# GpSimd sums for the last product of two memory layers, and new orders in the memory and last layers of a transformer kernel

## What is computed

```python
def memory_cross_attention(h, mem, wq, wkv, wo):
    q = (h @ wq).reshape(b, s, MEM_HEADS, MEM_HEAD_DIM)          # 4 heads of 256
    kv = (mem @ wkv).reshape(b, m, 2, MEM_HEADS, MEM_HEAD_DIM)
    k, v = kv[:, :, 0], kv[:, :, 1]
    sc = jnp.einsum('bqhd,bkhd->bhqk', q, k).astype(jnp.float32) * (MEM_HEAD_DIM ** -0.5)
    p = jax.nn.softmax(sc, axis=-1).astype(v.dtype)
    o = jnp.einsum('bhqk,bkhd->bqhd', p, v).reshape(b, s, D_MODEL)
    return o @ wo
...
for l in range(DEPTH):
    mix = hybrid_mixer(h, w_in[l], ...)
    h = layer_norm(ALPHA * h + mix, ln_g[l, 0], ln_b[l, 0])
    xa = memory_cross_attention(h, mem, mem_wq[l], mem_wkv[l], mem_wo[l])
    h = layer_norm(ALPHA * h + xa, ln_g[l, 1], ln_b[l, 1])
    f = swiglu(...) if l % 2 == 0 else moe_swiglu(...)
    h = layer_norm(ALPHA * h + f, ln_g[l, 2], ln_b[l, 2])
...
for layer in range(DEPTH):
    y = even_mixer(rmsnorm(x, pre_norm[layer]), ...) if layer % 2 == 0 else odd_mixer(...)
    x = x + rmsnorm(y, post_norm[layer])
```

## Time and profile before

| what | value |
|---|---|
| median of 3 runs (2184.64 to 2188.2) | 2184.92 us |
| the profiled execution | 2184.75 us, its span 2183.0 us |
| PE busy | 2119.3 us, 97% of the span, 13136 records (two for each matmul) |
| DVE, ACT, POOL busy | 677.9, 296.4, 64.9 us |
| granted clock of PE over the span | 0.993 |
| DMA | 485.52 MB, 222 GB/s on average |
| idle of PE in front of instructions | 14.5 us behind the norms of L1576, none other over 4.8 |

### The profile page before, as it was taken

How to read it: one execution, slowest core, us unless ns; L and a number is a source line. 1 busy time by engine, 2 the same in 40 slices (tenths; PEclk the granted TensorE clock), 3 DMA queues, 4 the chain that set the end, 5 groups by cost and what they waited for, 6 DMA issues and landing times.

```text
span 2183.0 us, 29181 instructions
## 1 busy us (share of the span) xinstructions
PE 2119.3 (97%) x13136; PEld 1240.2 (57%) x13136; DVE 677.9 (31%) x1278; ACT 296.4 (14%) x635; POOL 64.9 (3%) x70
## 2 busy tenths in 40 slices
PE   7999999999999999989999999999999899999997
PEld 3887675998458766743333334333333454755986
DVE  2413212455632241232101001111000389344445
ACT  1242001111103310010000000000000032330100
POOL 0000000000000000000000000000000025000000
PEclk9999999999999999989999999999999999999999
DMA  7523532544335244146999998799999832316340
GB/s 283 226 78 139 208 120 86 219 155 157 124 134 198 97 174 174 39 173 247 385 399 382 399 394 359 290 400 384 399 391 397 342 135 97 109 70 246 116 155 20
DMA packets 38000, 485.52 MB, mean 222 GB/s; under 512 B 4288, under 2 KB 4320, under 8 KB 6768
## 3 DMA queue, kind: packets, MB, share of 16 engines
q1 hardware_dynamic: 34544, 465.70, 53.5%
q0 software_dynamic: 3328, 17.90, 2.1%
HBM read 482.53 MB, written 1.05 MB: 222 GB/s over the span
## 4 chain that ended last, share of the span: by engine, by line
PE 95%; DVE 3%; DMA 1%; ACT 1%; issue 0%; DVEq 0%; SPq 0%
PE bank L362 51%; PE pair L362 44%; DMA weights<-in_w_in 0%; DVE att L1515 0%; DMA norm_par<-in_norms 0%; DVE hT L1515 0%; ACT hT L2545 0%; DVE att L2262 0%; ACT big L2529 0%; DVE stats L1567 0%; DVE h L1576 0%; DVE weights L2014 0%; DVE big L1515 0%; DVE h L1574 0%; DVE big L2244 0%
## 5 line engine op out<-in xcount | busy, mean ns | idle before, releaser
L362 PE MATMUL bank<-weights,att 128*32 128x512 f32 (+1 forms) x4228 | 459.6, 593 | 0.0
L362 PEld LDWEIGHTS bank<-weights,att 128*32 128x32 f32 (+1 forms) x4228 | 135.8, 110 | 307.4 <-issue 307.4
L362 PE MATMUL pair<-weights,big 128*32 128x512 f32 (+2 forms) x1654 | 249.1, 584 | 2.2 <-issue 2.2
L362 PE MATMUL bank<-hT,weights 128*128 128x256 f32 (+1 forms) x1168 | 239.1, 363 | 0.0
L362 PEld LDWEIGHTS bank<-hT,weights 128*128 128x128 f32 x1168 | 204.6, 190 | 31.4 <-issue 8.0
L362 PEld LDWEIGHTS pair<-weights,big 128*32 128x32 f32 (+1 forms) x1654 | 93.4, 122 | 146.1 <-issue 144.0
L362 PE MATMUL pair<-weights,hT 128*128 128x512 f32 (+2 forms) x400 | 167.5, 579 | 3.1 <-DMA weights<-in_w_in 1.6
L1910 DVE TENSOR_TENSOR big<-head_gain,bank 128x256 f32<-128x256 f32 x66 | 27.8, 421 | 423.9 <-ACT head_gain L2706 423.9
L362 PE MATMUL pair<-hT,weights 128*128 128x128 f32 (+1 forms) x976 | 154.6, 319 | 4.8 <-DVE hT L1515 3.9
L362 PEld LDWEIGHTS pair<-hT,weights 128*128 128x128 f32 x976 | 142.0, 194 | 16.6 <-DVE hT L1515 4.4
L362 PEld LDWEIGHTS pair<-weights,hT 128*128 128x128 f32 x400 | 76.5, 192 | 90.2 <-issue 86.2
(11 more groups left out here) (385 smaller groups left out, 1861.8 us busy)
## 6 DMA issues: line engine op xcount, KB each, us to landing
weights<-in_moe_up SPq DMA_DIRECT2D x88, 2048.0 KB, 10.6
weights<-in_moe_down SPq DMA_DIRECT2D x40, 2048.0 KB, 11.2
weights<-in_w_in SPq DMA_DIRECT2D x18, 2048.0 KB, 8.2
weights<-in_ffn_up SPq DMA_DIRECT2D x11, 2048.0 KB, 7.3
weights<-in_even_in SPq DMA_DIRECT2D x10, 2048.0 KB, 7.6
weights<-in_mem_wkv SPq DMA_DIRECT2D x8, 2048.0 KB, 7.3
weights<-in_odd_in SPq DMA_DIRECT2D x8, 2048.0 KB, 7.3
norm_par<-in_norms POOLq DMA_DIRECT2D x10, 1024.0 KB, 7.5
```

The lines of the kernel that those rows point to most:

```text
L362: ins = pe.matmul(o, lhsT, rhs, **flags)
```

## The change

1. In the memory layers kT1, v0, qT0 and qT1 are made by `seven_products`, with token sums in `prob` and `probT` and tile sums in the free part of `big`. hT is copied by ACT, not DVE. Scores wait for the half of qT that they need.
2. xo is made by `seven_rows`, whose seven sub-products have the rows as outputs; its token sums are made by DVE behind each head's value copy, and the sums over its two weight tiles by GpSimd (`xo_weight_sums`): eight subtractions of 128x1024, one after the other, from the end of qT1 on.
3. Its sums and norm are those of the dense layer's end, now a function (`rows_added`).
4. In the heads DVE's loop is written out, with the scaling of head 2 ahead of the value copy of head 0.
5. `few_sum` takes the last rows' statistics half by half.
6. Even layer: the turns and angles of step 0 come early, the scan's C is prepared in `prob` and `probT`, and two filler matmuls stand ahead of the wait for eu.
7. Odd layer: tile 14's sums are made once PE has finished the first half of c = 0, statistics and gain go by 256 columns, and for c = 1 the seventh sub-product has its own bank and is added ahead of the fourth.

```diff
...
+        xo_sums = [big_flat[:, 4096 + 2048 * i:6144 + 2048 * i].rearrange("p (r n) -> p r n", n=512) for i in range(3)]
+        xo_tokens = hT_flat.rearrange("p (i r t) -> p i r t", i=4, t=P)
...
-                for c in range(2):
-                    product_T(("kT", l, c), lambda kk: memT[:, kk, :], KD)
-                product(("v0", l), memT_at, KD, [512], KD)
+                product_T(("kT", l, 0), lambda kk: memT[:, kk, :], KD)
+
+                def memT_half(j, t):
+                    return lambda k: memT_at(KD // 2 * j + k, t)
+                seven_products(("kT", l, 1), memT_half, mem_sums, mem_tile_sums[1], first=True)
+                seven_products(("v0", l), memT_half, mem_sums, mem_tile_sums[0], by_token=True)
                 pe.wait_ge(*L.next("normed", 2))
-                transpose_rows(("hT", "mem", l), lambda t, kk: h[:, t, kk * P:(kk + 1) * P], KD)
-
-                pe.wait_ge(*emptied((("hT", "mem", l), KD - 2)))
-                for c in range(2):
-                    product_T(("qT", l, c), lambda kk: hT[:, kk, :], KD)
-                pe.wait_ge(*emptied(("qT", l, 1)))
+                transpose_rows(("hT", "mem", l), h_at, KD)
+                pe.wait_ge(*emptied((("hT", "mem", l), 2)))
+                seven_products(("qT", l, 0), hT_half, mem_sums, mem_tile_sums[1], first=True,
+                               second=lambda: pe.wait_ge(*emptied((("hT", "mem", l), KD - 2))))
+                seven_products(("qT", l, 1), hT_half, mem_sums, mem_tile_sums[0])
 
                 last_v = product_in_steps(("v", l), memT_at, KD, [512], 2)
 
                 def values(i):
                     def v(j):
+                        if (i, j) == (0, 0):
+                            pe.wait_ge(*emptied(("v0", l)))
                         if (i, j) == (MEM_HEADS // 2, 0):
                             pe.wait_ge(*emptied((("v", l), 0)))
                         return memory[:, j, i * MEM_HD:(i + 1) * MEM_HD]
                     return v
                 heads(("x", l), [([(hv[:, 2 * i + j, :], hv[:, 8 + 2 * i + j, :]) for j in range(2)],
-                                  values(i), MEM_HD, False) for i in range(MEM_HEADS)], last_v)
+                                  values(i), MEM_HD, False) for i in range(MEM_HEADS)], last_v,
+                      before=lambda i: pe.wait_ge(*emptied(("qT", l, i // 2))) if i in (0, 2) else None)
                 pe.wait_ge(*emptied((("x", l), "value", 3)))
-                product_rows(("xo", l), yT_at)
+                seven_rows(("xo", l), yT_at, xo_sums, xo_tokens, "xo_sums_ready")
...
+            def seven_rows(name, rows, sums, tokens_of, ready):
+
+                outs = rows_accumulators(name)
+                left, right = next_tile(), next_tile()
+                lt, rt = [weights[:, s, :].rearrange("p (r k n) -> p r k n", k=2, n=512) for s in (left, right)]
+                for i in (1, 2, 6, 5, 3, 7, 4):
+                    if i == 6:
+                        pe.wait_ge(*L.next(ready))
+                        pe.wait_ge(*L.next("xo_weights_ready"))
+                    for r in range(4):
+                        a11, a12, a21, a22 = [rows(2 * r + x, t) for t in range(NT) for x in range(2)]
+                        s1, s2, s3, s4 = [tokens_of[:, x, r, :] for x in range(4)]
+                        t1, t2, t4 = [t[:, r, :] for t in sums]
+                        tokens, block = {1: (a11, lt[:, r, 0, :]), 2: (a12, lt[:, r, 1, :]), 3: (s4, rt[:, r, 1, :]),
+                                         4: (a22, t4), 5: (s1, t1), 6: (s2, t2), 7: (s3, rt[:, r, 0, :])}[i]
+                        ins = mm(outs[i], tokens, block, start=(r == 0), stop=(r == 3))
+                    end_late(ins, (name, i))
+                    if i == 2:
+                        slot_owed[0] = f"slot{left}_used"
+                slot_owed[0] = f"slot{right}_used"
...
+                filling[0] = ("scan", 0)
+                fill(2)
...
-                    fill(4)
+                    fill(4 if b else 2)
...
+                    seventh = begin(banks, ("do", c, "seventh"), late=True)[:, 0:256] if c else last[:, 0:256]
...
+                                elif i == 4:
+                                    ins.then_inc(sems("do_half_done"), 1)
...
+                base = (first_ffn_tile + HID_CHUNKS + len(FEW_DOWN) if l else 0) + first_mem_tile
+
...
+                def summed(src):
+                    sums_of_tokens(src, mem_sums).then_inc(sems("token_sums_ready"), 1)
+                    L.passed("token_sums_ready")
+
+                def ahead(i):
+                    return lambda: sums_of_tile(tile(i), mem_tile_sums[i % 2])
+                memT = big_flat[:, 2048:4096].rearrange("p (k t) -> p k t", t=T)
+                ve.wait_ge(*emptied((("memT", l), KD - 2)))
+                ahead(1)()
+                summed(memT)
+                copy(("kT", l, 0), hv[:, 8:12, :].rearrange("p (a b) t -> p a (b t)", a=2))
+                crossed_tile(("kT", l, 1), mem_kept, lambda t, i: hv[:, 12 + 2 * i:14 + 2 * i, t * P:(t + 1) * P], ahead(2))
+                crossed_tile(("v0", l), mem_kept, lambda t, i: memory[:, t, 256 * i:256 * i + 256], ahead(3))
+                ve.wait_ge(*emptied((("hT", "mem", l), KD - 2)))
+                summed(hT)
+                crossed_tile(("qT", l, 0), mem_kept, lambda t, i: hv[:, 2 * i:2 * i + 2, t * P:(t + 1) * P], ahead(4))
+                crossed_tile(("qT", l, 1), mem_kept, lambda t, i: hv[:, 4 + 2 * i:6 + 2 * i, t * P:(t + 1) * P])
+                def token_sums_of(m):
+
+                    a11, a12, a21, a22 = [yT[:, 2 * m + x, t * P:(t + 1) * P] for t in range(NT) for x in range(2)]
+                    s1, s2, s3, s4 = [xo_tokens[:, i, m, :] for i in range(4)]
+                    link(ve.tensor_tensor(s1, a21, a22, ALU.add))
+                    link(ve.tensor_tensor(s2, s1, a11, ALU.subtract))
+                    ve.tensor_tensor(s3, a11, a21, ALU.subtract)
+                    return ve.tensor_tensor(s4, a12, s2, ALU.subtract)
 
                 def store(name, m):
                     copy(name, yT[:, 2 * m:2 * m + 2, :], lambda o: o[:, :].rearrange("p (k t) -> p k t", t=T))
-                heads(("x", l), MEM_HEADS, store, MEM_HD ** -0.5)
-                residual_norm(("xo", l))
+                    ve.wait_ge(*emptied(name))
+                    ins = token_sums_of(m)
+                    if m == MEM_HEADS - 1:
+                        ins.then_inc(sems("xo_sums_ready"), 1)
+                        L.passed("xo_sums_ready")
+                name = ("x", l)
+                heads_max(name, 0, MEM_HD ** -0.5)
+                heads_max(name, 1, MEM_HD ** -0.5)
+                heads_scaled(name, 0)
+                heads_max(name, 2, MEM_HD ** -0.5)
+                heads_scaled(name, 1)
+                heads_scaled(name, 2)
+                store((name, "value", 0), 0)
+                heads_max(name, 3, MEM_HD ** -0.5)
+                heads_scaled(name, 3)
+                for m in range(1, MEM_HEADS):
+                    store((name, "value", m), m)
+                rows_added(("xo", l), norm_slot(), ALPHA)
...
             def few_sum(g, row=None):
...
+                        if row is not None:
                             ve.wait_ge(*emptied(("few_sum", g, i, t)))
+                            ins = ve.bn_stats(stats[:, t, i, :], hc)
...
+            def rows_added(name, par, alpha=1.0):
 
...
-                def add(t, c, src, done=link):
-                    done(ve.tensor_tensor(part(t, c), part(t, c), src, ALU.add))
+                def add(t, c, src, done=link, scale=1.0):
+                    done(ve.scalar_tensor_tensor(part(t, c), part(t, c), scale, src, ALU.mult, ALU.add))
 
...
                 x, k1 = d_kept
...
-                row_norm(0, g, b)
-                add(1, 1, second[:, 0, :], freeing("B"))
-                ve.wait_ge(*filled((name, "down", 7)))
+                row_norm(0, *par)
+                add(1, 1, second[:, 0, :], freeing("B"), scale=alpha)
+                ve.wait_ge(*filled((name, 7)))
                 freeing(7)(ve.tensor_tensor(x, x, p7, ALU.add))
                 add(1, 1, x)
                 ve.bn_stats(stats[:, 1, 1, :], part(1, 1))
-                add(1, 0, x)
-                ve.wait_ge(*filled((name, "down", 4)))
+                add(1, 0, x, scale=alpha)
+                ve.wait_ge(*filled((name, 4)))
                 add(1, 0, p4, freeing(4))
                 link(ve.bn_stats(stats[:, 1, 0, :], part(1, 0)))
-                row_norm(1, g, b)
+                row_norm(1, *par)
...
+                ve.wait_ge(*L.next("do_half_done"))
+                sums_of_tile(odd_tile(14), do_tile_sums[0], "do_sums_ready")
...
+                    else:
+                        measured(0, c, 1)
...
+                        ve.wait_ge(*filled(("do", c, 7)))
+                        seventh, _ = bank(("do", c, "seventh"))
```

(39 more changed lines are left out.)

257 lines of the change are left out of this document (128 added, 129 removed).

## The result

The changed kernel takes 2162.03 us (median of 4 runs, 2160.9 to 2163.08) beside 2185.39 us for the kernel before (4 runs, 2184.64 to 2188.2): a ratio of 0.9891, 95% interval 0.9874 to 0.9908, so 23.4 us less. The forecast was 2156.2 with a range of 2150 to 2168. Direction and range held; 5.8 us of the expected gain are missing. (The profiled execution of the changed kernel, 2160.9 us, was its quickest; that is the other 1.1.)

What follows compares the result with a forecast made beforehand. TensorE (PE) was taken as the bound, 95% of the chain that ended last. Memory layers 25.4, less 4.0 for GpSimd's contention, plus 0.6, 2.1 and 4.4, made 28.5 us off 2184.75: 2156.2 us, range 2150 to 2168.

Steps and rivals of the forecast that it cites:

- Products and gaps ahead of the heads: Memory layers before the scores: seven products save 1.25 us each on kT1, qT0, qT1 and 1.65 on v0; gaps shrink too.
- The gap before qT: Memory layer, between v0 and qT: 1.8 us gained of the 1.96 us gap on VectorE.
- xo: Last product of each memory layer: 28 matmuls in place of 32, saving 3.45 us.
- The gaps in the heads: Memory layer, end of the heads: of gaps of 1.58 and 0.78 us, 1.3 gained.
- The sums by GpSimd: Memory layers: subtractions hidden from xo, but holding up VectorE in the heads 0 to 6 us a layer; 4.0 lost in all.
- three signs of being wrong: Memory layers: GpSimd's rows over 4.7 us, heads taking more than 34 us, or the clock falling inside the heads.
- first rival: Heads: every small VectorE instruction waits for a whole GpSimd one, 6 us a layer, clock falls too; 2168 us, chance 0.20.
- third rival: Whole kernel: no contention between GpSimd and VectorE, all gaps gone; 2150 us, chance 0.08.
- the second row's norm: After xo: norm takes about 5.8 us against 4.75, a gap of 2.7 before the second router transposes; 1.1 lost once.
- The expert layer's end: Last rows' statistics taken as each half is added: 0.6 us gained of PE's gap of 4.81.
- the even layer: Its start: the 2.31 us wait for eu goes, VectorE and GpSimd then bind the scan; 2.1 us gained (0.9 to 4.2).
- the last layer: The 2.68 us gap goes and the work behind the last matmul falls from 5.35 to 3.6 us; 4.4 gained.

Runs made afterwards that it cites:

- e10: The changed kernel with kT1, v0, qT0 and qT1 as before (eight products, hT copied by VectorE, scores waiting for all of qT): 2177.01 us.
- e1: The changed kernel with GpSimd's eight subtractions per memory layer left out, so some of xo's sub-products multiply other numbers: 2150.73 us.
- e6: The changed kernel with the scaling of the maximum made by ScalarE instead of VectorE, GpSimd's sums where they were: 2151.21 us.
- e9: The changed kernel with GpSimd's sums as four subtractions of 128x2048 per memory layer, rows doubled: 2163.65 us.
- e4: The changed kernel with GpSimd's eight subtractions of 128x1024 cut into sixteen of 128x512: 2153.01 us.
- e5: The changed kernel run again unchanged, as the base on another chip: 2161.48 us, a ratio of 0.9877 to the kernel before.
- e3: The changed kernel with xo's weight sums made by VectorE instead of GpSimd, five within qT1's time, three behind head 0's maximum: 2150.08 us.
- e12: e3 with six more matmuls of 128x512, results overwritten, ahead of xo in the first memory layer: 2157.82 us.
- e8: The changed kernel with three orders as before (last statistics of the experts, even layer's start, last layer): 2170.06 us.
- e2: The changed kernel with GpSimd's sums begun one tile earlier, five beside qT1 and three behind it: 2150.89 us.

## Why the prediction was right in its direction and 5.8 us short

**Products and gaps ahead of the heads: right.** 12.5 and 12.09 us per tile, forecast 12.51 and 12.09; 8.89 us a layer, forecast 8.52. The gap before qT went whole (1.96, taken as 1.8). e10 prices both layers' products alone.

**xo: right** in its size (3.43, forecast 3.45), and its sums were ready in time: GpSimd ended at 335.6, xo's third sub-product began at 357.6, 22 us later. The rows took 2.35 us, forecast 2.24, far from the 4.7 at which PE would have waited.

**The gaps in the heads: 1.3 forecast, 1.86 measured** (32.16 before, 30.30 in e1).

**The sums by GpSimd: the step that failed is the price of what they do to VectorE.** Two of the prediction's three signs of being wrong came: the heads took 35.03 us, over its 34, and in the second layer the clock fell inside them (below). That the time lies in the range does not make this step right. The working had all parts: two waits per head if the scaling of the maximum waits too, 1.5 us spare, 0 to 6 a layer. It then took 2, "nearer the lower end, as the row with two inputs is the only kind the trace shows waiting". Measured is 4.73 a layer in the first (30.30 in e1, 35.03 with the sums; the gaps are 4.29 of it, the rest is the overlap of matmuls lost at each stop). e6 shows that one term: without the small instruction nearly the whole loss goes, though prob still waits 2 us. The two waits add up, and a fixed amount of the sum is spare:

| head | wait of the small one | wait of prob | sum | PE's gap | spare |
|---|---|---|---|---|---|
| changed kernel, head 1 | 2.01 | 2.16 | 4.17 | 2.51 | 1.66 |
| changed kernel, head 2 | 1.28 | 2.16 | 3.44 | 1.78 | 1.66 |
| e9, head 1 | 1.48 | 4.31 | 5.79 | 4.13 | 1.66 |
| e10, head 1 | 0.43 | 2.17 | 2.60 | 0.94 | 1.66 |
| e4, head 1 | 0.37 | 1.08 | 1.45 | none | |
| e5, second layer, head 2 | 2.05 | 0 | 2.05 | 0.35 | 1.70 |
| changed kernel, second layer, head 2 | 0 | 1.96 | 1.96 | 0.31 | 1.65 |

A wait is the instruction's length less its length undisturbed, 0.17 or 0.69. The estimate of 1.5 spare was close, and one wait per head, as the forecast had it, costs 0.3 to 0.5 us; the second wait is what it left out. So the right reading was close to the first rival's condition (every small instruction waits for a whole GpSimd one; the tensor_scalar does, the reciprocal does not), at 4.7 a layer instead of its 6, and the measured 2162 lies in the span of that rival, 2160 to 2168, to which I gave 0.20, above the 2152 to 2160 of the forecast. The lack of a row for an instruction was taken as a reason for the low end, and it is none. The third rival, without contention, had 2150 us; the kernels in which VectorE waits for nothing take 2150.1 to 2150.9 (e1 to e3).

The rule of the Trainium skill that the prediction cited (SBUF — State Buffer, Who interferes with whom) names tensor_scalar among the instructions that can take the pair of ports shared with GpSimd, and tensor_reduce as one that never contends. The rows agree on both: 2.18 instead of 0.17 for the one, 0.69 as always for the other. The reduction reads PSUM here, though, so its row does not tell the kind of instruction from the place of its input.

**The clock: not in the forecast.** A granted clock of 0.50 is the lower of its two levels, 1.2 GHz in place of 2.4. In the dense layer and the mixer behind it 1.73 went so (e12), and e5, the same kernel once more, lost it again (1.70). At the second row's norm: the gap before the second router transposes is 2.73 us, as forecast (1.16 more), but the clock was down at 952 us, before PE resumed, while in the kernel before it fell only once PE had resumed (0.53 from 970 to 972), and the other 1.13 of the stretch went there. In e5 that stretch lost 1.11 in all, so this part comes and goes between executions of one kernel. The row of PE's timeline, changed kernel:

```profile
952.96 1.97 PE L375 MATMUL bank<-const,h 128*128 128x128 f32 x8 [2.73 <-DVE h L1626]
```

and the stretch, with the columns of e12's:

```profile
952.00:972.00 20.00, 13.66 (x44) 10.51 (x45) 11.33 (x49) 3.97 (x5) 0.57 (x1) 0.50 0.37 155
```

In the second layer's heads the clock fell behind the gap of 2.51 (0.53 from 902 to 904), so the scores came later and the small instruction fell clear of GpSimd's rows, and the second gap is 0.31 instead of 1.78: the layer came out the same, 9.44 beside 9.45 in the first. And the even layer's first product gained 1.0 at its start, where the fall ahead of it was shorter; in e5 the even layer gained 2.2 in all, so this part is not the change's either.

**The expert layer's end, the even layer, the last layer: right.** 0.66, 2.0 and 4.66 (e8), forecast 0.6, 2.1 and 4.4. As forecast, the even layer's scan is bound by VectorE and GpSimd, and PE waits for GpSimd before the last outputs; in the last layer there is no gap, and 3.7 us stand behind the last matmul (2150.43 + 1.89 = 2152.32 to 2154.75 + 1.28 = 2156.03), before 5.4. The changed kernel's timeline of PE:

```profile
1719.86 2.34 PE L375 MATMUL bank<-const,att 128*128 128x128 f32 x8 [4.15 <-DVE h L1997]
...
1841.03 1.06 PE L375 MATMUL pair<-probT,att 128*32 128x256 f32 x8 [1.90 <-POOL probT L3039]
...
2150.43 1.89 PE L375 MATMUL bank<-probT,big 128*128 128x256 f32 x8
```

VectorE's last row:

```profile
2154.75 1.28 DVE L2498 SCALAR_TENSOR_TENSOR h<-big,rstd,h 128x1024 f32<-128x1024 f32 x1
```

**The sum, put right.** Forecast 28.5; less 4.4 in the heads, less 1.7 and 1.2 in the two stretches behind xo, plus 0.8 ahead of the heads, 1.0 in the even layer and 0.9 in all the rest (0.6 of it ahead of the first memory layer, where nothing was changed): 23.9.

## What to carry to other kernels

Before work goes to GpSimd, list which instructions of VectorE on the path run beside it, the smallest too: an instruction of 0.17 us that can wait for a whole GpSimd row waits as long as a large one. Add up the waits between two points where PE needs VectorE and take off what is spare; only the rest costs time. Then move the GpSimd work to where VectorE only reads PSUM or is idle (e2), cut it so that a wait fits into the slack (e4), or move the one small instruction (e6): each gave back 8 to 11 us here, 1.7 of it by the clock in the dense layer. Where a gap of some 2 us is opened or shifted in a PE-bound kernel, put the clock into the range: an estimate from the falls here (1.1 and 1.7 us) is 1 to 2 us for each such gap.

## What was not expected of the hardware

- The fall of TensorE's clock goes with where in time a gap lies, not with its length alone: a gap of 2.22 us cost 1.7 us more where PE resumed at 520.9 to 522.9 us and nothing in ten other kernels, while a gap of 4.13 us in e9's heads was followed by 0.50 in both layers, and the gap of 2.51 in the changed kernel's heads by 1.00 in the first layer and 0.53 in the second. Shifting a kernel by 5.2 us of useless matmuls made it fall in the dense layer, which took 1.7 us more (e12).
- GpSimd's subtraction took 4.50 us for 128x2048 (e9), 2.35 for 128x1024, 1.26 for 128x512 (e4), nearly in proportion. It was itself held up little by VectorE: by up to 0.34 us a row, where VectorE's prob ran at its start (2.68 in the changed kernel, 1.60 in e4, 4.84 in e9).
- VectorE's prob of 0.69 us took 1.77, 2.85 and 5.00 beside GpSimd's rows of 128x512, 128x1024 and 128x2048; its tensor_scalar of 128x2 took up to 2.22, its reciprocal of 128x2 no more than 0.15 (e6).
